# Block-triangular inverse in a chunked RWKV7 recurrence: 4x4 starting blocks with a VectorE transpose, in place of 2x2 blocks and a fifth doubling level

## What is computed

```python
def step(state, inp):
    r_t, w_t, k_t, v_t, an_t, b_t = inp
    sa = jnp.einsum('bhij,bhj->bhi', state, an_t)
    state = (state * w_t[:, :, None, :] + sa[..., None] * b_t[:, :, None, :]
             + v_t[..., None] * k_t[:, :, None, :])
    return state, jnp.einsum('bhij,bhj->bhi', state, r_t)
```

## Time and profile before

| | us |
|---|---|
| median of 3 runs | 4765.99 |
| the 3 runs | 4753.48 to 4782.15 |
| profiled execution, its own time | 4792.91 |
| its span, first to last instruction | 4791.1 |
| mean granted TensorE clock (share of full) | 0.927 |
| recurrence, about | 1742 to 2820 |

### The profile page before, as it was taken

The page is one execution under the profiler, slowest core; times in us unless marked ns, Lnnn a source line. Parts: engine busy times, 40 slices in busy tenths (PEclk is TensorE's granted clock), DMA queues, the critical chain, the costliest instruction groups (busy, mean ns, idle before and its releaser), DMA issues. The chain is left out here.

```text
span 4791.1 us, 126596 instructions
## 1 busy us (share of the span) xinstructions
PE 4243.0 (89%) x52302; PEld 3847.6 (80%) x52302; DVE 2931.6 (61%) x5154; ACT 2233.5 (47%) x4176; POOL 1173.7 (24%) x954
## 2 busy tenths in 40 slices
PE   6979999986999968888888869963999999999998
PEld 5869999965888856666666647752999999999998
DVE  6879999954888854444444437757444444444443
ACT  4568888844666633333333322210444444444443
POOL 4544444421434420100001213301112112112110
PEclk9989999966999979999888979975999999999999
DMA  8920000004444332222222236712556556556554
GB/s 168 185 56 25 25 22 23 25 28 125 148 150 144 131 128 63 69 63 62 59 61 61 63 81 201 208 59 63 169 174 175 173 174 177 176 174 175 171 174 106
DMA packets 555367, 540.97 MB, mean 113 GB/s; under 512 B 80320, under 2 KB 502464, under 8 KB 554944
## 3 DMA queue, kind: packets, MB, share of 16 engines
q1 hardware_dynamic: 489920, 435.51, 29.3%
q0 software_dynamic: 14784, 46.57, 4.7%
q10 hardware_dynamic: 50240, 52.44, 4.6%
HBM read 377.99 MB, written 156.43 MB: 112 GB/s over the span
## 5 line engine op out<-in xcount | busy, mean ns | idle before, releaser
L2269 DVE TENSOR_TENSOR g_wlo<-g_raw,g_whi 128x2048 fp32r<-128x2048 f32 x192 | 439.2, 2287 | 115.3 <-ACT g_whi L2231 115.3
L2231 ACT ACTIVATE g_whi<-g_raw 128x2048 fp32r<-128x2048 f32 x192 | 366.9, 1911 | 145.1 <-DMA g_raw<-expert_w_gate 145.1
L2340 PE MATMUL g_pD<-g_whi,g_hh 128*128 128x256 f32 x1536 | 417.5, 285 | 2.5 <-ACT g_o L2258 2.4
L2340 PE MATMUL g_pD<-g_wlo,g_hh 128*128 128x256 f32 x1536 | 408.4, 279 | 0.0
L1362 ACT ACTIVATE d_y<-d_pB 128x256 f32<-128x256 f32 x480 | 184.4, 384 | 441.5 <-PE d_pB L1547 441.5
L1119 PE MATMUL c_pP<-c_xh,c_whi 128*128 128x258 f32 x1120 | 329.8, 294 | 36.0 <-DMA c_gup<-g_lora_up 29.6
L587 DVE TENSOR_TENSOR sapl<-sapT,saph 128x512 fp32r<-128x512 f32 x512 | 329.8, 686 | 2.7 <-ACT saph L546 2.7
L577 DVE TENSOR_REDUCE sanm<-sapS 128x1 f32<-128x1024 f32 x256 | 313.5, 1225 | 26.5 <-PE sapS L628 16.5
L1340 POOL TENSOR_TENSOR d_kr<-d_kr,d_fixed 128x512 f32<-128x512 f32 x80 | 101.8, 1272 | 923.8 <-ACT d_kr L1366 923.8
L546 ACT ACTIVATE saph<-sapT 128x512 fp32r<-128x512 f32 x512 | 278.7, 596 | 94.3 <-PE sapT L640 94.3
L2202 POOL DMA_INDIRECT g_x<-hn_rows,index x48 | 69.4, 1445 | 1030.7 <-PE g_pU L2324 1020.4
(11 more groups left out here) (364 smaller groups left out, 12635.4 us busy)
## 6 DMA issues: line engine op xcount, KB each, us to landing
g_raw<-expert_w_gate SPq DMA_DIRECT2D x64, 1024.0 KB, 5.1
g_raw<-expert_w_up SPq DMA_DIRECT2D x64, 1024.0 KB, 7.0
g_raw<-expert_w_down SPq DMA_DIRECT2D x64, 1024.0 KB, 5.1
ops<-c_ops SPq DMA_DIRECT2D x40, 1024.0 KB, 4.2
d_bd<-ops SPq DMA_DIRECT2D x160, 256.0 KB, 3.1
c_xh<-xT_hi SPq DMA_DIRECT2D x10, 1032.0 KB, 6.5
c_xl<-xT_lo SPq DMA_DIRECT2D x10, 1032.0 KB, 8.5
x_in<-x SPq DMA_DIRECT2D x20, 512.0 KB, 7.6
```

The lines of the kernel that those rows point to most:

```text
L2231: act.activation(w_hi[:, Q % NBUF, :, :], raw[:, Q % NRAW, :, :], ACT.Copy).then_inc(s["g_hi"], 1)
L2269: dve.tensor_tensor(w_lo[:, Q % NBUF, :, :], raw[:, Q % NRAW, :, :], w_hi[:, Q % NBUF, :, :].bitcast(F32), ALU.subtract).then_inc(s["g_lo" ...
L2340: mm = pe.matmul(pD[k][:, 0:WB], x[:, d, k * P:(k + 1) * P], w[:, b, d, :], start=(d == 0 and i == 0), stop=(d == DC - 1 and i == len(part ...
```

## The change

The starting blocks are 4x4. A strictly triangular 4x4 block has L^4 = 0, so (1 + L)(1 + L^2) is its inverse. VectorE masks `left` to 4x4 blocks (`few`, L), adds the identity (`one_few`, 1 + L) and turns `few` in 32x32 blocks (`fewT`). TensorE squares (`squared`, 8 matmuls, in place of `x3`), VectorE adds the identity (`odd`), TensorE multiplies (`fours`, 8 matmuls, at l = 0), and ScalarE copies the product into Z. Four levels follow in positions l = 1 to 4; a step still has 6 slots. The waits of `between`, `through`, `solved`, `out` and `state` are renumbered for the moved levels.

```diff
-LEVELS = [2, 4, 8, 16, 32]
+BASE = 4
+LEVELS = [4, 8, 16, 32]
 NL = len(LEVELS)
-LATE = (NL + 1) // 2
+STEPS = NL + 2
+LATE = STEPS // 2
...
+            def fours(m, par, g):
+
+                act.wait_ge(of[g]["fix"], m + 1)
+                act.activation(Z[par][g][:], grow[g], ACT.Copy).then_inc(of[g]["init"], 1)
...
             def reads(m, par, g):
                 dve.wait_ge(of[g]["x1"], m + 1)
+                dve.tensor_tensor(few[g][:], left[g][:, :, 0:C], bc(beside[:, g, 0:1, :], [P, RT, C]), ALU.mult).then_inc(of[g]["few"], 1)
                 dve.tensor_tensor(br[par][g][:], left[g], bc(upon[:, g:g + 1, :], [P, RT, 2 * C]), ALU.mult).then_inc(of[g]["br"], 1)
-
-            def smallest(m, par, g):
-
-                dve.wait_ge(of[g]["x3"], m + 1)
-                dve.tensor_tensor(Z[par][g][:], grow[g], bc(beside[:, g, 0:1, :], [P, RT, C]), ALU.mult).then_inc(of[g]["in"], 1)
-                dve.wait_ge(of[g]["in"], m + 1)
-                dve.tensor_tensor(Z[par][g][:], Z[par][g][:], bc(ident, [P, RT, C]), ALU.add).then_inc(of[g]["init"], 1)
+                dve.wait_ge(of[g]["few"], m + 1)
+                dve.transpose(fewT[g][:].rearrange("p j t -> p (j t)"), few[g][:].rearrange("p j t -> p (j t)")).then_inc(of[g]["turn"], 1)
+                dve.tensor_tensor(one_few[g][:], few[g][:], bc(ident, [P, RT, C]), ALU.add).then_inc(of[g]["one"], 1)
+
+            def smallest(m, g):
+
+                dve.wait_ge(of[g]["sq"], m + 1)
+                dve.tensor_tensor(odd[g][:], grow[g], bc(ident, [P, RT, C]), ALU.add).then_inc(of[g]["odd"], 1)
...
-            def x3(m, par, g):
+            def squared(m, g):
+                pe.wait_ge(of[g]["turn"], m + 1)
                 if m:
                     pe.wait_ge(of[g]["Yc"], yc(m - 1, NL))
-                for q, a, h in HEADS:
-                    mm = solve(at(grow[g], a, h, q), op(par, g, OP_A, q, a, h), op(par, g, OP_B, q, a, h))
-                mm.then_inc(of[g]["x3"], 1)
+                for h in range(2):
+                    for q in range(2):
+                        for a in range(2):
+                            mm = solve(at(grow[g], a, h, q), at(few[g], a, h, q), at(fewT[g], a, h, q))
+                mm.then_inc(of[g]["sq"], 1)
+
+            def fours(m, g):
+
+                pe.wait_ge(of[g]["one"], m + 1)
+                pe.wait_ge(of[g]["odd"], m + 1)
+                for h in range(2):
+                    for q in range(2):
+                        for a in range(2):
+                            mm = solve(at(grow[g], a, h, q), at(one_few[g], a, h, q), at(odd[g], a, h, q))
+                mm.then_inc(of[g]["fix"], 1)
...
                 if part == 0:
-                    if l < NL and is_chunk(m):
-                        stationary(m, par, l, g)
-                        between(m, par, l, g, m - 1)
+                    if l == 0 and is_chunk(m):
+                        fours(m, g)
+                    if 0 < l <= NL and is_chunk(m):
+                        stationary(m, par, l - 1, g)
+                        between(m, par, l - 1, g, m - 1)
...
```

More of the change, by code:

```diff
@@ L1216, in recurrence @@
         two = lambda n, shape: [[sb(f"d_{n}{k}{g}", shape) for g in range(2)] for k in range(2)]
+        one_g = lambda n: [sb(f"d_{n}{g}", [P, RT, C]) for g in range(2)]
         br, kr = [two(n, [P, RT, 2 * C]) for n in "br kr".split()]
         tbk = two("tbk", [P, 2, RT, C])
+        few, fewT, one_few, odd = [one_g(n) for n in ("few", "fewT", "one", "odd")]
         Z, Y, tv, st, y_out = [two(n, [P, RT, C]) for n in "z y tv st yo".split()]
@@ L1223, in recurrence @@
         pA, pB = [[ps(f"d_p{n}{g}", (P, RT, 256)) for g in range(2)] for n in "AB"]
-        each = "la0 la1 lb0 lb1 yst0 yst1 x1 x3 x2c bk bkc br mask in init P Pe Z Ze T Yc zs zkc zsc u uc yo yac ye sn tmp S".split()
+        each = "la0 la1 lb0 lb1 yst0 yst1 x1 x2c bk bkc br mask few turn one sq odd fix init P Pe Z Ze T Yc zs zkc zsc u uc yo yac ye sn tmp S".split()
         s = sems("d_id d_dm d_z d_seen d_wo d_wohi d_wolo")
@@ L1267, in step @@
             def step(n, par, i):
-                for k in range(NL + 1):
+                for k in range(STEPS):
                     for part in range(2):
@@ L1385, in turned @@
                 act.activation(tv[par][g][:], right[g][:, 0:2, :].rearrange("p q (h t) -> p q h t", h=2), ACT.Copy).then_inc(of[g]["bkc"], 1)
+            def fours(m, par, g):
+                act.wait_ge(of[g]["fix"], m + 1)
+                act.activation(Z[par][g][:], grow[g], ACT.Copy).then_inc(of[g]["init"], 1)
             def run(m, par, i, l, part, g):
                 if part == 0:
-                    if is_chunk(m):
-                        stationary(m, par, l, g)
-                    if l == NL and is_chunk(m + 1):
+                    if l == 0 and is_chunk(m):
+                        fours(m, par, g)
+                    if l > 0 and is_chunk(m):
+                        stationary(m, par, l - 1, g)
+                    if l == STEPS - 1 and is_chunk(m + 1):
                         keys(m + 1, 1 - par, g)
@@ L1399, in run @@
                         read(m - 1, g)
-                    if l == NL - 1 and is_chunk(m):
+                    if l == 4 and is_chunk(m):
                         turned(m, par, g)
@@ L1472, in run @@
                 if part == 0:
-                    if l < NL and is_chunk(m):
-                        between(m, l, g)
-                    if l == NL and is_chunk(m + 1):
+                    if 0 < l <= NL and is_chunk(m):
+                        between(m, l - 1, g)
+                    if l == STEPS - 1 and is_chunk(m + 1):
                         reads(m + 1, 1 - par, g)
@@ L1483, in run @@
                         state(m - 1, 1 - par, g)
[L1484 to L1487, removed]
+                    if 0 < l <= NL and is_chunk(m):
+                        grown(m, par, l - 1, g)
+                    if l == STEPS - 1 and is_chunk(m + 1):
+                        smallest(m + 1, g)
             reads(0, 0, 0)
-            smallest(0, 0, 0)
+            smallest(0, 0)
             order(dve, staggered(run))
@@ L1587, in through @@
                 if n + 1 < NCH:
-                    pe.wait_ge(of[g]["Pe"], NL * (n + 1) + 1)
+                    pe.wait_ge(of[g]["few"], n + 2)
+                    pe.wait_ge(of[g]["br"], n + 2)
+                    pe.wait_ge(of[g]["x2c"], n + 2)
                 for h in range(2):
@@ L1602, in solved @@
                 if n + 1 < NCH:
[L1603 removed]
+                    pe.wait_ge(of[g]["Pe"], NL * (n + 1) + 1)
                 for h in range(2):
@@ L1625, in state @@
             def state(n, par, g):
-                pe.wait_ge(of[g]["Pe"], NL * (n + 1) + 3 + 1)
+                pe.wait_ge(of[g]["Pe"], NL * (n + 1) + 2 + 1)
                 for q in range(2):
@@ L1635, in run @@
                 if part == 0:
-                    if l < NL and is_chunk(m):
-                        stationary(m, par, l, g)
-                        between(m, par, l, g, m - 1)
[L1639 to L1643, removed]
+                    if l == 0 and is_chunk(m):
+                        fours(m, g)
+                    if 0 < l <= NL and is_chunk(m):
+                        stationary(m, par, l - 1, g)
+                        between(m, par, l - 1, g, m - 1)
+                    if l == STEPS - 1 and is_chunk(m + 1):
+                        x12(m + 1, 1 - par, g)
+                    if l == STEPS - 1 and is_chunk(m):
+                        stationary(m, par, NL, g)
                 else:
@@ L1652, in run @@
                         state(m - 1, 1 - par, g)
[L1653 to L1659, removed]
+                    if l == 4 and is_chunk(m):
+                        turned(m, par, g)
+                    if 0 < l <= NL and is_chunk(m):
+                        grown(m, par, l - 1, g)
+                    if l == STEPS - 1 and is_chunk(m + 1):
+                        squared(m + 1, g)
             x12(0, 0, 0)
-            x3(0, 0, 0)
+            squared(0, 0)
             step = staggered(run)
@@ L2430, in mask_table @@
     for d in range(2):
-        for m in [1] + LEVELS:
+        tabs.append((p // BASE == t // BASE) & (t > p if d == 0 else p > t))
+        for m in LEVELS:
             tabs.append((p // (2 * m) == t // (2 * m)) & (t // m % 2 == d) & (p // m % 2 == 1 - d))
```

10 lines of the change are left out of this document (5 added, 5 removed).

## The result

The changed kernel takes 4750.01 us (median of 17 runs, 4728.75 to 4764.85) against 4775.59 us for the kernel before (17 runs beside it): a ratio of 0.9946, 95% interval 0.9928 to 0.9965. Measured a second time it was 0.9937 (0.9911 to 0.9964). So the change makes the kernel faster by about 0.55%, 26 us, where I had forecast +7 us and no measurable change.

What follows compares the result with a forecast made beforehand. The prediction took the recurrence to be bound by a fixed order in which TensorE waits for VectorE's Z, plus "issue" gaps. Clean step +17, half clock -6 and code -4 gave +7 on 4766: 4773 us, range 4700 to 4820.

Steps and rivals of the forecast that it cites:

- the term "Code": TensorE's unrolled program in the recurrence: 5% fewer matmuls cut the some 75 us of "issue" waits, -4 us.
- The clean step: A recurrence step at full clock: VectorE's new ops make it 0.45 us longer, 37 steps, +17 us.
- second half: Group 1's `x12` to group 0's next, at full clock: `br` and what follows come 0.34 later, net +0.25 us.
- first half: Group 0's `x12` to group 1's, at full clock: VectorE's new ops delay masking, `out` and T, net +0.20 us.
- Point (2) of what would show it: In the profile after, T's wait longer for VectorE and TensorE's busy share in the stage falls below 0.83.
- At half clock: Steps at 1.2 GHz, where TensorE hardly idles: its removed work counts, -1 to -15 us, taken as -6.
- The faster rival: TensorE's order is the bound and VectorE's new ops are hidden: 4694 us, half of it 4733; chance 0.26.
- The clock rival: More TensorE idle time lowers its clock; time at half clock grows by half, +37 us, 4810; chance 0.20.
- The transpose: VectorE's transpose, taken as 0.42 us; the rival has it slow or `one_few` meeting GpSimd, +44 us, 4817; chance 0.09.

Runs made afterwards that it cites:

- before_short: The kernel before with 7 of the 8 matmuls of `x3` left out for all but the first two chunks; ratio 0.9941.
- pad9: The changed kernel with 9 extra one-column matmuls (36 TensorE instructions) per group and chunk; ratio 1.0039 to the kernel before.
- pad27: The changed kernel with 27 extra one-column matmuls (108 TensorE instructions) per group and chunk; ratio 1.0295.
- late_blocks: The changed kernel with `br` masked first, transpose and `one_few` behind the other group's masking, squaring and `fours` moved later; ratio 0.9918, again 0.9922.
- late_two: late_blocks with `fours` behind `through` and, for group 0, `one_few` ahead of the transpose; ratio 0.9939.
- late_short: late_two with 7 of the 8 matmuls of `squared` and of `fours` left out for all but the first two chunks; ratio 0.9900.

## Why the prediction was wrong

The kernels on one scale (records of the stage by 125; "issue" and time at half clock in the stage, the latter summed from the clock records; ratio to the kernel before):

| kernel | records / 125 | "issue", us | half clock, us | ratio |
|---|---|---|---|---|
| before | 220 | 79, 75 | 218, 209 | 1 |
| before_short | 212 | 54 | 240 | 0.9941 |
| after | 209 | 59, 53 | 201, 160 | 0.9946, 0.9937 |
| pad9 | 220 | 74 | 237 | 1.0039 |
| pad27 | 243 | 109 | 457 | 1.0295 |
| late_blocks | 209 | 58, 61 | 198, 218 | 0.9918, 0.9922 |
| late_two | 209 | 62 | 196 | 0.9939 |
| late_short | 192 | 26 | 283 | 0.9900 |

**The step that failed is the term "Code", -4 us.** I took the 75 us of waits as proportional to the code, 5% of them for 5% of it. The runs show that they are not: 11 blocks fewer take 21 us away (1.9 us each), 8 fewer in before_short take 23 (2.8 each), 11 more than after in pad9 add 18 (1.6 each), 34 more in pad27 add 53 (1.6 each), 17 fewer than late_two take 36 (2.1 each). The average over 220 blocks is 0.35 us, but most blocks come in time and cost nothing: a wait of over 0.3 us stands at 64 and 67 of them before, and at 52 and 48 after. A marginal block costs some 2 us. The term measures -21 us.

**The clean step was right in mechanism, and its size too large.** Forecast +0.20 and +0.25; the shortest halves measure +0.06 and +0.12, the medians nothing, so 0 to +7 us in place of +17. In the second half T to T shortened by 0.19, where I had 0.09; in the first T came at 4.10, not 4.2. The halves that I forecast, 12.6 and 10.8, started from a first half of 12.42. Point (2) of what would show it holds by half: in front of T TensorE waits for VectorE 74 and 75 us in the stage, as the 74 us before, and `squared` waits for the transpose another 20 and 23. TensorE's share of the stage stayed at 84%, though, since it now has less idle time in gaps.

**At half clock**, -6 forecast. The stage lost 23 us, the waits on "issue" took 21, the clean step gave 0 to +7: -2 to -9 is left for this and for the clock. The time at half clock fell from 218 and 209 us to 201 and 160, by 33 on average, which at 0.34 each is already 11. But two profiles of the changed kernel differ by 41 us in it. No run separates the two, so the size of this term stays open.

**The faster rival gave the right side for the wrong reason.** It needed T of group 1 at or before its old place and a shorter wait in front of the next T; in the clean step shown T came later (4.10 against 3.75) and the wait was longer (0.77 against 0.59 on the PE rows). That TensorE's queue is not the bound of the second half is shown by pad9, which left it at 10.66. The right side of the forecast would have come by luck here. **The clock rival** didn't come about in the change (0.90 and 0.92 for 0.90), but does in late_short and, mostly behind late code, in pad27. **The transpose** took 0.43 (I took 0.42), and `one_few` 0.38 clear of GpSimd by 0.44 us (forecast 0.45). In late_blocks, where it wasn't, it cost the forecast 1.3.

Which block comes late, and why a step shortened on VectorE's side brings 0 to 0.3%, is open: that it only meets the late code sooner fits late_two, but "issue" rose by 3 to 9 us, less than the 20 that are missing. The fastest version that computes everything is late_blocks, 0.9918 and 0.9922; its intervals overlap those of the change.

## What to carry to other kernels

Where an engine's program is unrolled, count its instructions as a cost of their own: read the waits on "issue" summed over all lines, see whether they stand a fixed number of instructions apart, and price a removed block at what a marginal one costs (here some 2 us, and more with the clock that a wait takes along), not at the average. A dose experiment tests it in two runs: pad with instructions that do next to nothing, and leave some out of the old kernel. A hand-made timeline of one clean step can be right to about a tenth of a microsecond at each point and still miss the result, if the clean steps aren't where the time changes.

## What the runs showed of the hardware

- TensorE's waits on "issue" stand at multiples of 125 matmul records (124, 125, 125, 374, 375, 499, 501 in seven windows), 16.4 KB of code by the instruction queue's packets, and are up to 3.3 us long. In pad27, the longest program, 49 of the 71 distances between such waits of over 0.3 us are three blocks (375 to 377 records). Leaving out the 320 stores did not shorten them (52 against 53 to 59 us).
- A group of 8 fp32 matmuls on 64x64 tiles that uses two of the four positions takes longer than one that uses all four, in which output and input halves are combined in all ways. `x3` of the kernel before, and `squared` above at 1868.08 with the same shapes:

```profile
2745.76 0.46 PE L1510 MATMUL d_pB<-d_bd 64*64 64x64 f32 x16
```

  0.46 against 0.68 us from first start to last end. The rise of 0.22 is what the prediction made of the Trainium skill's rule (TensorEngine Tiling (Array Packing), Tiling Modes and Key Properties): the trace agrees. Both groups lay in waits, so it cost nothing at full clock.
- VectorE's transpose of 128x256 fp32 in 32x32 blocks takes 0.43 us (80 of them, 434 to 436 ns), as long as an elementwise op of that size.
- Both more and fewer instructions went with less clock: 108 nearly empty ones more per group and chunk moved the stage's clock from 0.90 and 0.92 to 0.81, most stretches at half clock behind waits on "issue"; 56 fewer moved it from 0.90 to 0.86 (late_two to late_short), most of them not behind such a wait.
